# A decoder layer with an expert ring on one Trainium2 core: a constants tensor narrowed by 96 columns, and the working memory moved to a start at a multiple of 512 bytes

## The chip, the cores and the metric

The kernel runs on one core of a Trainium2 chip. The metric is the device time of one execution in microseconds. Three executions of the kernel before took 1125.96 us as the median, 1125.75 us the shortest and 1127.47 us the longest.

## The reference

The reference is one layer of a hybrid decoder for 256 tokens of width 1024, in float32. Three branches are computed from one projection of the normalised input (a sparse attention of 8 heads with an indexer that picks 64 keys per query, an RWKV-7 time mixing of 8 heads, and a cross-attention into 256 memory tokens), merged by sigmoid gates and added to the input. Then comes the part in which the kernel spends more than half of its time, a feed-forward layer of 16384 single-neuron experts. For each token and each of 8 heads it picks 16 experts, 128 per token:

```python
def peer_ffn(xn, w_q, key1, key2, u, v):
    q = (xn @ w_q).reshape(B, S, PEER_HEADS, 2, PEER_QDIM // 2)
    s1 = jnp.einsum('bshd,kd->bshk', q[..., 0, :], key1)     # 128 keys
    s2 = jnp.einsum('bshd,kd->bshk', q[..., 1, :], key2)
    v1, i1 = lax.top_k(s1, 16); v2, i2 = lax.top_k(s2, 16)
    cand = v1[..., :, None] + v2[..., None, :]
    sc, ci = lax.top_k(cand.reshape(..., 256), 16)
    expert = e1 * PEER_KEYS + e2                             # from i1, i2 at ci
    gate = jax.nn.softmax(sc, axis=-1)
    ue, ve = u[expert], v[expert]                            # rows of 1024
    hid = jax.nn.gelu(jnp.einsum('td,ted->te', xn, ue))
    return jnp.einsum('te,ted->td', gate * hid, ve)
```

## The kernel before, in words

The program has two stages. In the first, TensorE works through the projections: 51 weight blocks of 1 MB each, loaded by SyncE into a ring of three buffers (`wring`) and a few spare places, and between them the small matmuls of the three branches, in an order written out by hand (`SCHEDULE`). The blocks are used by `channels` (L610), `tokens` (L623) and `up` (L959); all are matmuls of 128x128 weights with 256 columns.

In the second stage (heads 0 to 7 of the experts, for two tiles of 128 tokens) the unit of work is one gather. GpSimd issues an indirect DMA (L1835) that fetches for each of the 128 tokens one row of the table `experts`, in which `u` and `v` of an expert stand side by side: 2048 floats, 8192 bytes, into that token's partition of one of 8 slots. There are 16 experts x 8 heads x 2 tiles = 256 such gathers. When one has landed, VectorE makes the dot product of the `u` half with the token (L1769, in place), ScalarE the gelu (L1265), the product with the gate (L1269) and a diagonal matrix of the weights (L1272), and TensorE multiplies that with the `v` half and sums in PSUM (L991). Then the slot is free (`group_free`) and GpSimd issues the next gather into it. Between the dots VectorE chooses the experts of the next head.

No pool hands out the memory. Each tensor is allocated once, one behind the other in every partition, in the order of the code: `const`, `vec`, `trig`, `lora`, `glora`, `rows`, `small`, `ones`, `pos_i`, `pool_mem`. Each start is rounded up to a multiple of 32 bytes, and `const` starts at byte 16512. The last one, `pool_mem` (47872 columns of float32), holds everything else: the function `part(at, ...)` cuts tiles from it by hand, with `K1 = 256` columns as the unit, so that the weight buffers, the slots of the ring of rows (`slot`) and the output buffer (`o_sb`) all begin at a multiple of 1024 bytes from its start:

```python
RING0 = Q0 + 16 * K1
slot = [part(RING0 + BLOCK * i, BLOCK) for i in range(SLOTS)]
```

`const` holds the constant matrices side by side; `CONST[name]` is the pair of first column and width by which `c(name)` finds them. Two of them, `pick_pairs` and `pick_ones`, serve the sums of squares (`square_sums`, L642 to L645). Each is 224 columns wide, with the values in columns 96 to 127 and zeros left and right, and the four matmuls of a sum read windows of 128 columns that start at 96, 64, 32 and 0. `small` holds single columns, of which the first 144 are used.

Of the kernel before, what the change touches and what calls it, by code (L numbers as in the profile page):

```python
# [13 lines left out]
P = 128  # L14
# [53 lines left out]

CONST = {}
_c = 0  # L70
for _name, _n in [("ident", 128), ("headsel", 2), ("pick_pairs", 224), ("pick_ones", 224), ("rot", 128), ("causal", 128),
                  ("gram_mask", 4 * CHUNK), ("level", CHUNK * LEVELS), ("iota", 16), ("inv_freq", 1), ("two_idents", CHUNK), ("to_heads", W)]:
    CONST[_name] = (_c, _n)
    _c += _n
CONST_COLS = _c


VEC = {}
# [8 lines left out]
def constants():  # L87

    p = np.arange(P)
    out = {}  # L90
    out["ident"] = np.eye(P)
    out["pick_pairs"] = np.zeros((P, 224))
    out["pick_pairs"][:, 96:128] = p[:, None] // HD == np.arange(32)[None, :] // 16
    out["pick_ones"] = np.zeros((P, 224))
    out["pick_ones"][:, 96:128] = 1.0
    out["to_heads"] = p[:, None] == 16 * (np.arange(W)[None, :] // HD)
    out["two_idents"] = np.concatenate([np.eye(64), np.eye(64)])
    rot = np.zeros((P, P))
    for base in (0, HD):
        for i in range(8):  # L100
            rot[base + 8 + i, base + i] = -1.0
            rot[base + i, base + 8 + i] = 1.0
    out["rot"] = rot
    out["causal"] = np.where(p[None, :] <= p[:, None], 0.0, OFF)
    s, t = p[:, None] % CHUNK, np.arange(CHUNK)[None, :]
    strict, incl = s < t, s <= t
    out["gram_mask"] = np.concatenate([strict, incl, strict, incl], axis=1)
    out["level"] = np.concatenate(
        [(s // (2 << l) == t // (2 << l)) & ((t >> l) % 2 == 1) & ((s >> l) % 2 == 0) for l in range(LEVELS)], axis=1)
    out["headsel"] = (p[:, None] // HD == np.arange(2)[None, :])  # L110
    out["iota"] = np.tile(np.arange(16), (P, 1))
    inv = (np.float32(1.0) / (np.float32(500000.0) ** (np.arange(0, 16, 2, dtype=np.float32) / np.float32(16))))
    col = np.zeros(P)
    for q in range(P):
        if q % HD < 16:
            col[q] = inv[(q % HD) % 8]
    out["inv_freq"] = col[:, None]
    return np.ascontiguousarray(np.concatenate([out[n] for n in CONST], axis=1).astype(np.float32))
# [87 lines left out]
def build(nc, t_in, out):  # L206
    ctx = ExitStack()
    with ctx:
        def sb(name, shape, dt=F32):
            return ctx.enter_context(nc.sbuf_tensor(name, shape, dt))  # L210
# [4 lines left out]

        const = sb("const", [P, CONST_COLS])
        vec = sb("vec", [P, VEC_COLS])
# [1 line left out]
        lora = sb("lora", [P, W])  # L219
        glora = sb("glora", [P, W])  # L220
        rows = sb("rows", [P, 2 * W])
        small = sb("small", [P, 160])
        ones = sb("ones", [P, P])
        pos_i = sb("pos_i", [P, S], I32)
        pool_mem = sb("pool_mem", [P, POOL_COLS])
# [146 lines left out]
        def c(name):  # L372
            a, n = CONST[name]
            return const[:, a:a + n]
# [5 lines left out]
        ident = c("ident")  # L380
# [1510 lines left out]
```

## Time and profile before

| | |
|---|---|
| median of 3 runs | 1125.96 us |
| the profiled execution | 1125.06 us |
| its span, first to last instruction | 1123.2 us |
| TensorE (PE) busy | 879.6 us, 78% |
| VectorE (DVE) busy | 649.7 us, 58% |
| ScalarE (ACT) busy | 392.9 us, 35% |
| GpSimd (POOL) busy | 324.7 us, 29% |
| DMA | 329.78 MB, mean 294 GB/s |
| queue of the gathers (q0) | 36864 packets, 268.45 MB, 57.7% of 16 engines |
| mean granted TensorE clock | 0.848 |

The table is of the profiled execution except for its first line. Shares of the span are averages over two stages that have different limits, so they don't tell what bounds the kernel; the windows below do. A queue's share is the time that its packets took on the 16 DMA engines, as a part of 16 times the span or window. A packet here is one row, or the write of a semaphore at a transfer's end. Neighbouring packets overlap a little, and a share can pass 100%. Windows are in us from the start of the span.

### The profile page before, as it was taken

The page shows a single profiled execution, that of the slowest core. Times are in us where ns is not written, and L with a number is a line of the kernel's source. Part 1 is how long each engine was busy: PE and PEld are TensorE (multiplying, and loading weights), DVE is VectorE, ACT ScalarE, POOL GpSimd, SP SyncE. Part 2 cuts the span into 40 slices and gives each one's busy share as a digit, 9 for nine tenths or more (in the row PEclk, how much of TensorE's full clock was granted, in tenths as well). Part 3 has the DMA queues.
Part 4 walks back from the last instruction along what each step waited for, and adds up shares of the span by engine and source line. Part 5 has one row for each costly group of instructions (what it writes and reads, how often), then busy time and mean ns, then how long its engine had stood idle before and what let it go on. Part 6 is the DMA issues. An engine that isn't in the chain of part 4 may idle for free.

```text
span 1123.2 us, 16457 instructions
## 1 busy us (share of the span) xinstructions
PE 879.6 (78%) x5738; PEld 518.5 (46%) x5738; DVE 649.7 (58%) x1544; ACT 392.9 (35%) x1094; POOL 324.7 (29%) x294
## 2 busy tenths in 40 slices
PE   9999999999999989988856566565565667656655
PEld 8888888878888878855411111111111111111111
DVE  3442541296453241666577668668757766766874
ACT  2024133315321101244454344344434434434443
POOL 0000000020011000225444545454544454445441
PEclk9999999999999999999985866777667566667677
DMA  8343423322222254789999999999999999999997
GB/s 321 135 150 113 146 79 113 113 76 76 76 76 78 76 211 148 298 332 404 421 420 422 420 422 422 421 422 421 421 421 422 421 422 422 422 422 421 422 422 290
DMA packets 46579, 329.78 MB, mean 294 GB/s; under 512 B 5312, under 2 KB 5568, under 8 KB 6848
## 3 DMA queue, kind: packets, MB, share of 16 engines
q0 software_dynamic: 36864, 268.45, 57.7%
q1 hardware_dynamic: 9104, 58.91, 14.5%
q10 hardware_dynamic: 560, 1.70, 0.4%
q8 instruction: 36, 0.59, 0.2%
q14 instruction: 15, 0.12, 0.0%
HBM read 328.00 MB, written 1.05 MB: 293 GB/s over the span
## 4 chain that ended last, share of the span: by engine, by line
PE 48%; DMA 27%; DVE 11%; ACT 7%; issue 6%; POOL 1%; POOLq 0%; DVEq 0%; ACTq 0%
DMA pool_mem<-in_experts,pool_mem 27%; PE psum_proj L610 20%; PE psum_job L991 8%; PE psum_proj L623 5%; DVE pool_mem L1769 4%; PE psum_proj L959 3%; PE psum_job L839 3%; ACT L1265 1%; DVE pool_mem L1710 1%; ACT L1253 1%; POOL pool_mem L1835 1%; ACT pool_mem L1272 1%; ACT pool_mem L1269 1%; DVE pool_mem L1707 1%; PE psum_proj L1014 1%
## 5 line engine op out<-in xcount | busy, mean ns | idle before, releaser
L991 PE MATMUL psum_job<-pool_mem 64*64 64x512 f32 x2048 | 378.2, 849 | 222.6 <-ACT pool_mem L1272 222.4
L1835 POOL DMA_INDIRECT pool_mem<-in_experts,pool_mem x256 | 302.5, 1182 | 444.3 <-PE psum_job L991 286.0
L1769 DVE CUSTOM_DVE_ANT_0 pool_mem<-pool_mem 128x1024 f32<-128x1024 f32 x256 | 310.5, 1225 | 188.0 <-DMA pool_mem<-in_experts,pool_mem 186.8
L991 PEld LDWEIGHTS psum_job<-pool_mem 64*64 64x64 f32 x2048 | 86.4, 172 | 510.3 <-issue 509.9
L610 PE MATMUL psum_proj<-pool_mem 128*128 128x256 f32 x1120 | 247.9, 380 | 0.7 <-ACT pool_mem L1085 0.7
L610 PEld LDWEIGHTS psum_proj<-pool_mem 128*128 128x128 f32 x1120 | 211.1, 190 | 33.8 <-issue 5.9
L1265 ACT ACTIVATE pool_mem<-pool_mem 128x1 f32<-128x1 f32 x256 | 51.6, 202 | 291.3 <-DVE pool_mem L1769 290.7
L1818 POOL TENSOR_TENSOR pool_mem<-pool_mem,const 128x256 f32<-128x256 f32 x24 | 16.7, 716 | 332.9 <-DVE pool_mem L1573 273.1
L1272 ACT ACTIVATE pool_mem<-const,pool_mem 128x64 f32<-128x64 f32 x256 | 89.1, 348 | 26.5 <-PE psum_job L991 0.6
L1269 ACT ACTIVATE pool_mem<-pool_mem 128x1 f32<-128x1 f32 x256 | 75.4, 294 | 9.3
L623 PE MATMUL psum_proj<-pool_mem 128*128 128x256 f32 x256 | 56.3, 380 | 1.6 <-DVE pool_mem L1653 1.6
L623 PEld LDWEIGHTS psum_proj<-pool_mem 128*128 128x128 f32 x256 | 48.4, 190 | 8.3 <-DVE pool_mem L1653 2.0
L959 PE MATMUL psum_proj<-pool_mem 128*128 128x256 f32 x192 | 43.5, 383 | 0.7 <-ACT pool_mem L1203 0.7
L959 PEld LDWEIGHTS psum_proj<-pool_mem 128*128 128x128 f32 x192 | 35.8, 190 | 6.1 <-ACT pool_mem L1203 0.9
L1117 ACT ACTIVATE pool_mem<-psum_proj,vec 128x256 f32<-128x256 f32 x24 | 10.1, 470 | 75.5 <-PE psum_proj L610 75.5
L1328 DVE RECIPROCAL pool_mem<-pool_mem 128x256 f32<-128x256 f32 x5 | 8.6, 1739 | 47.8 <-ACT pool_mem L1058 45.8
L839 PE MATMUL psum_job<-pool_mem 64*64 64x64 f32 x896 | 30.0, 220 | 1.4 <-issue 0.6
L839 PEld LDWEIGHTS psum_job<-pool_mem 64*64 64x64 f32 x896 | 27.8, 135 | 4.6 <-issue 4.3
L1253 ACT ACT_TABLE_LOAD x17 | 21.8, 1283 | 2.0 <-DVE pool_mem L1733 1.7
L1265 ACT ACT_TABLE_LOAD x17 | 21.8, 1283 | 0.3
L1585 DVE TENSOR_TENSOR pool_mem<-pool_mem,psum_job 128x256 f32<-128x256 f32 x36 | 13.9, 419 | 12.5 <-PE psum_job L839 11.5
L1769 DVE DVE_READ_ACCUMULATOR2_ANT pool_mem<- 128x1 f32 x256 | 21.0, 82 | 0.0
(250 smaller groups left out, 731.5 us busy)
## 6 DMA issues: line engine op xcount, KB each, us to landing
pool_mem<-in_weights SPq DMA_DIRECT2D x51, 1024.0 KB, 4.8
pool_mem<-in_experts,pool_mem POOLq DMA_INDIRECT x256, 14.0
const<-in_const SPq DMA_DIRECT2D x1, 1033.5 KB, 15.0
pool_mem<-in_xT SPq DMA_DIRECT2D x1, 1024.0 KB, 4.9
pool_mem<-in_memT SPq DMA_DIRECT2D x1, 1024.0 KB, 11.2
pool_mem<-in_x ACTq DMA_DIRECT2D x1, 1024.0 KB, 7.6
rows<-in_rows SPq DMA_DIRECT2D x1, 512.0 KB, 16.6
pool_mem<-in_ffn_gain ACTq DMA_DIRECT2D x1, 512.0 KB, 8.3
```

The source lines that it names most:

```text
L610: ins = mm(o[:, m, :], lhsT=w[:, k, m * P:(m + 1) * P], rhs=src[:, k, :], start=(k == 0), stop=(k == KT - 1))
L623: ins = mm(o[:, t, :], lhsT=src[:, k, t * P:(t + 1) * P], rhs=w[:, k, :], start=(k == 0), stop=(k == KT - 1))
L839: ins = mm(o[b, CHUNK * i:CHUNK * i + CHUNK], lhsT=left[b, 4 * g + i, :], rhs=c("two_idents")[b] if right is None else right[b, 4 * g + i, ...
L959: ins = mm(o[:, m, :], lhsT=w[:, 4 * (u % 2) + k, m * P:(m + 1) * P], rhs=ys[u // 4][:, k, :], start=(k == 0), stop=(k == 3))
L991: ins = mm(sum_bank(t, d)[sum_strip(i, d), :], lhsT=diag[rows_, g % DIAGS, :], rhs=slot[g % SLOTS][rows_, D + 512 * d:D + 512 * d + 512], ...
L1253: A(gate_e[:, par, :], top[:, par, :], ACT.Exp, bias=gstat[:, par, 0:1], accum_out=gstat[:, par, 1:2]).then_inc(sg["gsum"], 1)
L1265: A(act_h[:, par, col], hid[:, par, col], ACT.Gelu).then_inc(sg["gelu_ok"], 1)
L1269: A(weight[:, par, col], act_h[:, par, col], ACT.Copy, scale=gate_e[:, par, col]).then_inc(sg["weighed"], 1)
L1272: A(diag[:, g % DIAGS, :], c("two_idents"), ACT.Copy, scale=weight[:, par, col]).then_inc(sg["diag_ok"], 1)
L1769: ins = V.tensor_tensor_reduce(u, u, xn_tok[:, t, :], 1.0, 0.0, ALU.mult, ALU.add, hid[:, par, s_:s_ + 1])
L1818: G_.tensor_tensor(LmT[:, gs, :], gram[:, gs, 0, :], level.unsqueeze(1).to_broadcast([P, 4, CHUNK]), ALU.mult).then_inc(sg["lm_ok"], 1)
L1835: G_.indirect_dma_start(slot[s_ % SLOTS], None, t_in["experts"], bass.IndirectOffsetOnAxis(ap=expert_i[:, par, s_:s_ + 1], axis=0)).then_i ...
```

## The change

The matrix `pick_pairs` takes up 128 columns of `const` in place of 224. Its zeros on the right are no longer stored: `pick_ones` stands right behind it and begins with 96 zero columns, and the entry of `CONST` is widened to 224 again after the columns have been counted. `const` shrinks from 2067 to 1971 columns. `small` grows from 160 to 208 columns, and the added ones aren't used. No instruction is added, removed or moved. The starts of the tensors in each partition, in bytes, by the widths and the rounding to 32:

| | before | after |
|---|---|---|
| `const` | 16512 | 16512 |
| `vec` | 24800 | 24416 |
| `trig` | 25152 | 24768 |
| `lora` | 27200 | 26816 |
| `glora` | 29248 | 28864 |
| `rows` | 31296 | 30912 |
| `small` | 35392 | 35008 |
| `ones` | 36032 | 35840 |
| `pos_i` | 36544 | 36352 |
| `pool_mem` | 37568 = 73 x 512 + 192 | 37376 = 73 x 512 |

```diff
--- before.py
+++ after.py
@@ -68,11 +68,12 @@
 
 CONST = {}
 _c = 0
-for _name, _n in [("ident", 128), ("headsel", 2), ("pick_pairs", 224), ("pick_ones", 224), ("rot", 128), ("causal", 128),
+for _name, _n in [("ident", 128), ("headsel", 2), ("pick_pairs", 128), ("pick_ones", 224), ("rot", 128), ("causal", 128),
                   ("gram_mask", 4 * CHUNK), ("level", CHUNK * LEVELS), ("iota", 16), ("inv_freq", 1), ("two_idents", CHUNK), ("to_heads", W)]:
     CONST[_name] = (_c, _n)
     _c += _n
 CONST_COLS = _c
+CONST["pick_pairs"] = (CONST["pick_pairs"][0], 224)
 
 
 VEC = {}
@@ -89,7 +90,7 @@
     p = np.arange(P)
     out = {}
     out["ident"] = np.eye(P)
-    out["pick_pairs"] = np.zeros((P, 224))
+    out["pick_pairs"] = np.zeros((P, 128))
     out["pick_pairs"][:, 96:128] = p[:, None] // HD == np.arange(32)[None, :] // 16
     out["pick_ones"] = np.zeros((P, 224))
     out["pick_ones"][:, 96:128] = 1.0
@@ -219,7 +220,7 @@
         lora = sb("lora", [P, W])
         glora = sb("glora", [P, W])
         rows = sb("rows", [P, 2 * W])
-        small = sb("small", [P, 160])
+        small = sb("small", [P, 208])
         ones = sb("ones", [P, P])
         pos_i = sb("pos_i", [P, S], I32)
         pool_mem = sb("pool_mem", [P, POOL_COLS])
```

## Rows read from the trace of the kernel before

**Rows 1.** Windows by stage; columns are named in the first line.

```profile
core 0: us, PE busy (x) PEld busy (x) DVE busy (x) ACT busy (x) POOL busy (x), PEclk, DMA share, GB/s
0.00:466.00 466.00, 450.80 (x3435) 390.08 (x3436) 197.26 (x407) 115.00 (x221) 23.30 (x40) 1.00 0.36 129
466.00:1115.00 649.00, 426.02 (x2288) 127.84 (x2288) 450.52 (x1134) 276.35 (x869) 301.41 (x255) 0.74 1.00 415
1115.00:1123.20 8.20, 2.77 (x16) 0.57 (x16) 1.93 (x3) 1.51 (x5) 0.00 (x0) 0.71 0.23 65
```

**Rows 2.** Page, part 2, DMA in 40 slices of the span.

```profile
DMA  8343423322222254789999999999999999999997
GB/s 321 135 150 113 146 79 113 113 76 76 76 76 78 76 211 148 298 332 404 421 420 422 420 422 422 421 422 421 421 421 422 421 422 422 422 422 421 422 422 290
```

**Rows 3.** DMA queues and issues, 600 to 1100 us.

```profile
q0 software_dynamic: 28870, 210.23, 101.0%
...
issues: line engine op xcount, KB each, median us to landing
pool_mem<-in_experts,pool_mem POOLq DMA_INDIRECT x200, 14.6
```

**Rows 4.** Waits, 600 to 1100 us.

```profile
engine line waited for: us in total, times, longest us
...
ACT pool_mem L1265 <- DVE pool_mem L1769: 256.3, 174, 3.9
POOL pool_mem L1835 <- PE psum_job L991: 221.5, 119, 4.6
...
DVE pool_mem L1769 <- DMA pool_mem<-in_experts,pool_mem: 134.3, 111, 1.3
```

**Rows 5.** DMA issues of the whole span: KB each, median us to landing.

```profile
pool_mem<-in_weights SPq DMA_DIRECT2D x51, 1024.0 KB, 4.8
...
const<-in_const SPq DMA_DIRECT2D x1, 1033.5 KB, 15.0
...
pool_mem<-in_x ACTq DMA_DIRECT2D x1, 1024.0 KB, 7.6
...
pool_mem<-in_ffn_gain ACTq DMA_DIRECT2D x1, 512.0 KB, 8.3
...
pool_mem<-in_keysT ACTq DMA_DIRECT2D x1, 128.0 KB, 8.2
```

**Rows 6.** Windows, steady part of the second stage.

```profile
600.00:1100.00 500.00, 311.86 (x1608) 69.15 (x1600) 357.42 (x909) 211.89 (x670) 239.20 (x200) 0.69 1.01 422
```

**Rows 7.** Tile const, 0 to 120 us: duration ns min/median/max, first and last start.

```profile
L645 PE MATMUL psum_job<-pool_mem,const x24: 379/379/454, 90.7 to 115.2; 128*128 128x256 f32 x24
...
L532 SPq DMA_DIRECT2D const<-in_const x1: 443/443/443, 3.9 to 3.9; - x1
L1368 DVE TENSOR_SCALAR trig<-trig,const x1: 353/353/353, 69.3 to 69.3; 128x256 f32<-128x256 f32 x1
```

**Rows 8.** Waits of PE, 0 to 476 us, the longest two.

```profile
PE psum_job L819 <- DVE pool_mem L1553: 2.2, 2, 1.1
PE psum_proj L623 <- DVE pool_mem L1653: 1.6, 1, 1.6
```

**Rows 9.** DMA queues, 403.5 to 409.2 us.

```profile
q10 hardware_dynamic: 560, 1.70, 74.4%
```

**Rows 10.** DMA queues, 803.5 to 811.5 us.

```profile
q1 hardware_dynamic: 303, 0.52, 17.2%
```

**Rows 11.** DMA queues, 15.7 to 17 us.

```profile
DMA packets 71, 0.56 MB, mean 432 GB/s; under 512 B 3, under 2 KB 3, under 8 KB 3
...
q1 hardware_dynamic: 71, 0.56, 102.5%
```

**Rows 12.** Page, part 5, the matmuls of 128x256 on pool_mem.

```profile
L610 PE MATMUL psum_proj<-pool_mem 128*128 128x256 f32 x1120 | 247.9, 380 | 0.7 <-ACT pool_mem L1085 0.7
...
L623 PE MATMUL psum_proj<-pool_mem 128*128 128x256 f32 x256 | 56.3, 380 | 1.6 <-DVE pool_mem L1653 1.6
...
L959 PE MATMUL psum_proj<-pool_mem 128*128 128x256 f32 x192 | 43.5, 383 | 0.7 <-ACT pool_mem L1203 0.7
```

## The prediction

> **What bounds the kernel now.** I read the windows by stage first, then the slices of the page, the DMA queues of a steady window, the waits of the same window, and last the rows of single transfers.
>
> The windows by stage [rows 1] show two programs one behind the other. Up to 466 us TensorE is busy 450.80 of 466 us at a granted clock of 1.00, and DMA is busy a third of the time: this stage is bound by TensorE. From 466 to 1115 us the share of the DMA engines is 1.00 and TensorE is busy 426 of 649 us. In the slices [rows 2] the GB/s stand at 420 to 424 from slice 18 on, with no dip: a resource at its cap. The last 8.2 us, from the last landing to the end, are dots, a matmul, a copy and a store.
>
> The second stage is the 256 gathers of expert rows (L1835). Each writes 128 rows of 8192 bytes, 1.0486 MB, into one of 8 slots of the ring. At 422 GB/s [rows 3] that is 2.485 us, and 256 x 2.485 = 636 us, all but 13 us of the stage. The waits [rows 4] agree: the dots on VectorE wait 134.3 us for the gathers' data, ScalarE waits for the dots, and GpSimd for a slot to come free. Such a loop of waits could also be a latency loop. What excludes it is the time from issue to landing: 14.6 us for a gather in the steady window [rows 3], against 4.8 us for a weight load of the same 1 MB alone in the queue [rows 5]. So a gather stands about 10 us in the queue behind others, and the engines could be slower by that much per slot before the DMA engines ran dry. By throughput VectorE has 357.42 of 500 us used and TensorE 311.86 [rows 6].
>
> So in the first stage a change counts if TensorE's matmuls change, and in the second only if the time of a DMA row changes.
>
> **The change part by part.** No engine gets another instruction, another order or another wait. What changes are the start addresses and the width of one load.
>
> 1. Addresses. The program's tensors stand one behind the other in each partition, each start rounded up to 32 bytes; `const` begins at byte 16512. By the widths of the code, `pool_mem` begins before at 37568 = 73 x 512 + 192, afterwards at 37376 = 73 x 512. All that is cut from it as a whole tile lies at a multiple of 1024 bytes from that start, so before the change each row of the ring, and of each weight block, begins 192 bytes past a multiple of 512 (and of 256); afterwards each begins at a multiple of 512. Every other tensor moves by 384 or 192 bytes, both multiples of 64, so nothing changes for what an engine sees within 64 bytes.
>
> 2. The load of `const` is 96 columns narrower: 128 x 384 bytes = 49 KB less of 1033.5 KB. At 422 GB/s that is 0.12 us less in front of the lora weights, the rows and the fourth weight block. `const` lands 15.0 us after its issue at 3.9 us and is first read at 69.3 us [rows 5, 7]; the longest total wait of TensorE up to 476 us is 2.2 us, for VectorE and not for a load [rows 8]. The cover is some 50 us deep: cost and gain 0. If that cover were gone, 0.12 us.
>
> 3. The shared zero columns. The four matmuls of each sum of squares read the same 128-column weights from `const`, with the same values (the last 96 columns of the `pick_pairs` window are now the first of `pick_ones`, zeros). L645 keeps its count and its 379 ns [rows 7]: 0.
>
> 4. What the 192 bytes cost a DMA row. This is the only term that can matter: 256 gathers x 128 rows / 16 engines = 2048 rows on each engine one behind the other, so 1 ns of a row is 2.05 us of the kernel. The trace has only the old place of `pool_mem`, so I ask how much of a packet's time isn't the bytes. In the steady window q0 has 28870 packets and 210.23 MB in 101.0% of 16 x 500 us = 8080 us. For the three late loads that ScalarE issues (q10, rows of 4096 and 1024 bytes: 560 packets, 1664 KB = 1.704 MB by their issues) it is 74.4% of 16 x 5.7 us = 67.9 us [rows 3, 5, 9]. Time = packets x f + bytes / r for both gives f = 7 ns and r = 26.7 bytes per ns. So a row of 8192 bytes is 307 ns of bytes and 7 ns that don't depend on size. Both groups go to `pool_mem`, so a price per 256 or 512 bytes crossed could still sit in r; a price per row sits in f.
>
> Is f, or a part of r, the price of the 192 bytes? Two rows say no. Stores of the first half of the output (q1 in 803.5 to 811.5 us, rows of 2048 bytes read from `pool_mem`): 17.2% of 128 us = 22.0 us for 303 packets and 0.52 MB [rows 10]; bytes at 26.7 take 19.6 us, which leaves 8 ns a packet, and 47 of the 303 are semaphore packets with 4 bytes, which cross no boundary. And the load of `const` itself, whose rows go to a start 128 bytes past a multiple of 256 and come from rows of 8268 bytes that begin anywhere in HBM: 71 packets, 0.56 MB in 102.5% of 16 x 1.3 us = 21.3 us [rows 11], 38.1 us per MB against 38.4 in the ring, equal within the rounding of 0.56. Three offsets (192 written, 192 read, 128 written from scattered starts), one price.
>
> The bounds of term 4: the nearest gain is all of f on the rows, 7 ns x 2048 = 14.3 us. The far one is the highest rate in any short window, 432 GB/s in that of `const`: 256 x 1.0486 MB at 432 in place of 422 is 621 for 636 us, 15 us, the same size. A loss is bounded by the same distance the other way, since nothing here shows a row dearer than those of the ring: 15 us at most, with nothing that speaks for it. I take 0, to which the rows on stores and on `const` are nearest.
>
> The Trainium skill speaks against my choice here ("DMA: Bandwidth & Descriptors", How a descriptor splits into AXI transactions): a descriptor that doesn't start at a multiple of 256 bytes first fetches the bytes from the boundary below, which cost beats. It says so of reads; the experts' rows are 8192 bytes wide and so begin aligned in HBM, and the stores, where SBUF is the side read, show no such extra. Carried over to writes it would be the rival A below. The same page (Where 436 GB/s comes from) puts the ceiling of the ports at 435.2 GB/s; if alignment alone led there from 422, the 636 us would shrink by 19 us, and the time be 1106.
>
> 5. What the addresses cost the engines. Matmuls 128x256 f32 take 380 ns with both operands in `pool_mem` (L610, L623) and 383 ns at L959 [rows 12]; with the weights in `const`, which begins at another offset, the median is 379 [rows 7]. So the place of an operand is worth -1 to +3 ns. I take 0. In the second stage engine times hide under the transfers (10 us, above).
>
> The sum: 0 + 0 + 0 + 0 + 0. The profiled execution took 1125.06 us (span 1123.2 and 1.9 around it), 0.9 under the median of the runs, 1125.96. So the profile of after should read 1123 and the median 1125.9.
>
> **The rivals.**
>
> A. A row that begins 192 bytes off carries those bytes, or one more transaction, and loses them now. 192 bytes at 26.7 bytes per ns are 7.2 ns, all of f: 2048 x 7.2 = 14.7 us, 1111 us. With one part-filled transaction more, say 2 to 3 ns, 4 to 6 us: 1121. For it: the second stage is bound by nothing else for 636 us, a gain would pass through (VectorE would go from 71% to 73% busy), and f in fact equals 192 bytes. Against it: the semaphore packets, the stores and the const rows.
>
> B. The row does get cheaper at the SBUF end, and something else sets its pace. The slots don't: 0.06 us less per gather against the 10 us that a gather spends in the queue. It would have to be the reading end, the memory with the experts: then a row stays at 310 ns, 1125.9. It differs from the forecast in cause and not in time.
>
> C. Slower: TensorE's operand reads get worse at the new starts. Place: the first stage, where TensorE is 97% busy and each ns is paid in full. Price: the 3 ns between L610 and L959 on 1120 + 256 + 192 matmuls of that shape, 4.7 us: 1130.7 us. It decides from 1.5 ns a matmul on (2.3 us). For it only that such a spread exists; against it the 379 ns with weights from `const`.
>
> D. The change does not do what it says, and `pool_mem` isn't at a multiple of 512 afterwards. By the sums of the widths it is. No time of its own: 1125.9.
>
> **How the numbers follow.** Forecast, with B and D, 0.69: 1125.9, own range 1124.2 to 1127.8 (the three runs before span 1125.75 to 1127.47). A in full 0.07 (1111), A in part 0.13 (1117 to 1123). C 0.11 (up to 1130.7). A measurement of this kernel can tell about 0.2%, 2.3 us. Faster by more than that: 0.07 + 0.13 = 0.20. Slower: C, 0.11. Within: 0.69. The range reaches down into the partial A, to 1119, and up into C, to 1128.5; it leaves out A in full, the lower end of A in part and the upper half of C, just under 0.2.
>
> **What would show it.** Right: q0 in 600 to 1100 us again near 28870 packets, 422 GB/s and 101% share; 14.6 us to landing; L610 at 380 ns; the stages cut at 466 and 1115 us. Rival A: more packets in the same window (a gather is 2485 - 8 x 7 = 2429 ns, so 28870 x 2485/2429 = 29540 for the whole of f), 432 GB/s, and the last landing ahead of 1115. C: the first gather later than 466 us, with L610 above 381 ns. Wrong altogether would be a q0 rate that moves by over 0.5% either way, for I take the place of the rows to be worth nothing.

## The result: 8 us less, and the profile after

The kernel after takes 1118.50 us (median of 4 runs, 1117.58 to 1119.20), the kernel before 1126.51 us (4 runs, 1125.75 to 1127.47). The ratio is 0.9928, with a 95% interval from 0.9911 to 0.9945: 0.7% faster. The forecast range ended at 1119.0, half a microsecond above. The profiled execution took 1118.73 us, its span is 1116.9 us.

The slices of the page of after, to be read against [rows 2]: the steady level of the DMA engines has gone from 420 to 422 up to 425 to 428 GB/s, and up to 466 us the mean is 129 GB/s in both. The slices there differ in detail, since they are a little narrower after and a load can fall on the other side of a cut.

```profile
DMA  8343323322211253789999999999999999999997
GB/s 324 133 151 113 137 90 113 114 71 82 77 63 67 100 188 136 275 346 396 427 426 427 428 428 427 427 428 427 425 428 426 426 428 427 427 427 427 427 427 290
```

The DMA queues and issues of after in 600 to 1100 us (packets, MB, share of 16 engines) answer to [rows 3]:

```profile
DMA packets 29557, 213.58 MB, mean 427 GB/s; under 512 B 3299, under 2 KB 3299, under 8 KB 3555
...
q0 software_dynamic: 29246, 212.96, 100.8%
...
pool_mem<-in_experts,pool_mem POOLq DMA_INDIRECT x201, 13.6
```

29246 packets passed where 28870 did, in a share that is 0.2 points smaller, and a gather lands after 13.6 us and not 14.6. That is a cheaper row and not a fuller queue: 500 us / 213.58 MB x 1.0486 MB (the bytes of a gather) is 2455 ns. The same window of before moved 210.84 MB in all (the stores included), so 2487 ns. The difference is 32 ns over 8 rows of an engine, 4.0 ns a row, and 4.0 x 2048 = 8.2 us, the measured gain.

The windows by stage of after, cut where its last gather landed, answer to [rows 1]:

```profile
core 0: us, PE busy (x) PEld busy (x) DVE busy (x) ACT busy (x) POOL busy (x), PEclk, DMA share, GB/s
0.00:466.00 466.00, 450.82 (x3432) 389.80 (x3433) 197.19 (x407) 114.52 (x220) 22.12 (x38) 1.00 0.36 129
466.00:1109.00 643.00, 428.85 (x2295) 128.42 (x2297) 449.69 (x1135) 276.82 (x870) 311.10 (x256) 0.73 1.00 419
1109.00:1116.90 7.90, 2.10 (x16) 0.37 (x16) 1.88 (x3) 1.43 (x4) 0.00 (x0) 0.84 0.23 67
```

The second stage takes 643 us by these cuts in place of 649. From the issue of its first gather to the landing of the last it is 642.9 us (466.0 to 1108.9) where it was 650.7 (464.6 to 1115.3): 7.8 us less. The span fell by only 6.3 in this pair of profiles because the first stage ended 1.4 us later. The `up` matmuls, 383 ns in [rows 12], ran 394 ns there:

```profile
L611 PE MATMUL psum_proj<-pool_mem 128*128 128x256 f32 x1120 | 247.9, 380 | 0.7 <-ACT pool_mem L1086 0.7
...
L624 PE MATMUL psum_proj<-pool_mem 128*128 128x256 f32 x256 | 56.3, 380 | 1.6 <-DVE pool_mem L1654 1.6
...
L960 PE MATMUL psum_proj<-pool_mem 128*128 128x256 f32 x192 | 45.2, 394 | 0.7 <-ACT pool_mem L1204 0.7
```

It isn't the addresses. The longest of the 192 took 631 ns against 483 before, at the same median of 379, and the granted clock in 402 to 405 us was 0.61, so for part of these 3 us it was at the lower level, 1.2 GHz in place of 2.4. In before it was 1.00 there, although TensorE was busy 3.7 of the 6 us ahead of it in both. Of the runs below, e1, f2, f3 and f6 show the same 394 ns. The others show 383, and among them is g3, whose tensors stand where those of after do.

### The profile page after: what moved, and what is told of

It reads as the page before. It is cut to its first block, busy times and chain, and to the rows that moved or that the text cites. A ratio compares the mean times of both kernels' runs of the same rounds, so it can differ in the third digit from the quotient of the medians.

```text
span 1116.9 us, 16457 instructions
## 1 busy us (share of the span) xinstructions
PE 881.8 (79%) x5738; PEld 518.6 (46%) x5738; DVE 648.8 (58%) x1544; ACT 392.8 (35%) x1094; POOL 333.2 (30%) x294
## 4 chain that ended last, share of the span: by engine, by line
PE 46%; DMA 35%; DVE 7%; issue 5%; ACT 5%; POOL 0%; POOLq 0%; ACTq 0%; DVEq 0%
DMA pool_mem<-in_experts,pool_mem 35%; PE psum_proj L611 20%; PE psum_job L992 5%; PE psum_proj L624 5%; PE psum_proj L960 3%; DVE pool_mem L1770 3%; PE psum_job L840 3%; ACT pool_mem L1273 1%; DVE pool_mem L1711 1%; ACT pool_mem L1270 1%; PE psum_proj L1015 1%; PE psum_job L631 1%; DVE pool_mem L1708 1%; PE psum_job L640 1%; PE psum_job L660 1%
## 5 line engine op out<-in xcount | busy, mean ns | idle before, releaser
L1836 POOL DMA_INDIRECT pool_mem<-in_experts,pool_mem x256 | 311.1, 1215 | 431.0 <-PE psum_job L992 269.5
```

Of the source, the lines that this page charges most:

```text
L1836: G_.indirect_dma_start(slot[s_ % SLOTS], None, t_in["experts"], bass.IndirectOffsetOnAxis(ap=expert_i[:, par, s_:s_ + 1], axis=0)).then_i ...
```

## The experiments

The diffs below are against the kernel after and show the lines that matter; `...` marks lines that are left out. The ratios and intervals are those on record and can differ by 0.1% from the quotient of the medians that stand beside them. The theory after the comparison was W: in a long stream of rows, one that doesn't begin at a boundary in the partition costs the writing side a fixed amount more. The rivals were: the cost grows with the bytes below the boundary (P), the other tiles' places (E) or the narrower constants (C) brought the gain, only GpSimd's queue pays (Q), and only a meeting with the engines' accesses costs (E2).

### e1_zeros_only: the shared zeros without the boundary

```diff
-        small = sb("small", [P, 208])
+        small = sb("small", [P, 160])
```

> The shared zero columns alone: small stays at 160 columns, so pool_mem begins at 37184 = 72 x 512 + 320, 64 bytes past a multiple of 256. Theory W (a ring row that doesn't begin at a boundary costs the write side a fixed amount more once the queues have been full for some 10 us): the narrower constants do nothing, and since the rows still begin off the boundary the time is that of before, 1126.5, with q0 at 422 GB/s in 600 to 1100 us and 14.6 us to landing. Theory P (the extra cost grows with the bytes below the boundary, here 64 in place of 192): a third of the cost stays, 8.0 / 3 = 2.7 us, so about 1121.2 and 425 to 426 GB/s. Theory C (the narrower const or any moved address is what helped): 1118.5.

Measured: 1127.34 us (10 runs) against 1126.97 (19 runs) of before, ratio 0.9998 (0.9985 to 1.0012). The narrower constants are worth nothing: C falls. The steady window shows the level of before, although the rows now stand 64 bytes past a multiple of 256 and not 192, so P falls as it was put, with a boundary of 256 or 512:

```profile
DMA packets 29177, 210.83 MB, mean 422 GB/s; under 512 B 3254, under 2 KB 3254, under 8 KB 3510
...
q0 software_dynamic: 28866, 210.22, 101.0%
```

### e2_base_256: a multiple of 256 that is none of 512

```diff
-        small = sb("small", [P, 208])
+        small = sb("small", [P, 144])
```

> As after, but small has 144 columns: pool_mem begins at 37120 = 72 x 512 + 256. If the boundary that counts is 256 bytes, the time is that of after, 1118.5 us at 427 GB/s. If it is 512 bytes, theory W gives 1126.5 at 422 GB/s, and a cost by the bytes below the 512 boundary would give more than before (256 against 192), about 1129.

Measured: 1118.77 us (4 runs), ratio to before 0.9928 (0.9901 to 0.9954), the time of after. A multiple of 256 suffices. Whether a multiple of 128 would do was not tried, since every ring off the boundary in these runs begins 64 or 80 bytes past one:

```profile
DMA packets 29558, 213.61 MB, mean 427 GB/s; under 512 B 3296, under 2 KB 3296, under 8 KB 3552
...
q0 software_dynamic: 29247, 213.00, 100.8%
```

### e3_ring_alone_on and e4_ring_alone_off: which tiles count

e3 has `small` of 160 columns, with `pool_mem` at 72 x 512 + 320. e4 has `small` of 208, with `pool_mem` at 73 x 512. Both have:

```diff
-POOL_COLS = 187 * 256
+POOL_COLS = 187 * 256 + 48
...
-        RING0 = Q0 + 16 * K1
+        RING0 = Q0 + 16 * K1 + 48
```

> pool_mem begins at 37184 (320 past a multiple of 512), but the 8 slots of the ring are moved by 48 columns = 192 bytes, so that they alone begin at a multiple of 512. Theory W: only the ring's rows count, 1118.5 us and 427 GB/s. Theory E (tiles that the engines read and write beside the transfers, such as xn_tok, diag or the choice's tiles, must stand well): the time of e1, near 1126.

> The reverse: pool_mem begins at a multiple of 512 as in after, the ring's slots alone stand 192 bytes past one. Theory W: the whole gain is gone, 1126.5 us and 422 GB/s. Theory E: 1118.5.

Measured: e3 1118.28 us (4 runs), ratio 0.9913 (0.9892 to 0.9934). e4 1126.64 us (10 runs), ratio 0.9999 (0.9987 to 1.0011). The slots of e3 stand at the bytes of those of after, those of e4 at the bytes of those of before, while the rest of `pool_mem` is off the boundary in e3 and on it in e4. So the 8 slots alone carry the whole effect in both directions: E falls. The steady windows of e3 and, behind it, of e4:

```profile
DMA packets 29553, 213.59 MB, mean 427 GB/s; under 512 B 3293, under 2 KB 3293, under 8 KB 3549
...
q0 software_dynamic: 29242, 212.98, 100.8%
```

```profile
DMA packets 29182, 210.87 MB, mean 422 GB/s; under 512 B 3255, under 2 KB 3255, under 8 KB 3511
...
q0 software_dynamic: 28871, 210.25, 101.0%
```

### f1_sp_off and f2_sp_on: plain loads from SyncE

```diff
...
-                        G_.indirect_dma_start(slot[s_ % SLOTS], None, t_in["experts"],
-                                              bass.IndirectOffsetOnAxis(ap=expert_i[:, par, s_:s_ + 1], axis=0)
-                                              ).then_inc(slot_in[s_ % SLOTS], 16)
...
+            for n in range(PEER_HEADS * TILES):
+                sp.wait_ge(sg["experts_ok"], n + 1)
+                for s_ in range(TOPK):
+                    sp.wait_ge(sg["group_free"], n * HEAD_GROUPS + s_ + 1)
+                    sp.dma_start(slot[s_ % SLOTS], t_in["experts"][P * s_:P * s_ + P, :]).then_inc(slot_in[s_ % SLOTS], 16)
```

The loops and the wait around GpSimd's call go with it. f1 has the ring moved by 48 columns as in e4, f2 has it as in after.

> The ring's slots 192 bytes past a multiple of 512 (as in e4), and the 256 gathers replaced by plain loads that SyncE issues, each of the same 128 consecutive rows of the table for a place in the ring; the rows fetched are not the chosen ones, and both stores wait to the end. It asks whether the cost belongs to GpSimd's indirect DMAs or to any queue that is kept full. Theory W (any long stream of rows off the boundary pays, short bursts don't because the write side can fall some 100 ns behind first): the steady rate is 422 GB/s, rows of 312 to 319 ns. Theory Q (only the software queue pays): 427 GB/s and 309 ns as in every weight load of before.

> f1 with the ring at a multiple of 512. Both theories: 427 GB/s and rows of 309 ns; what counts is the difference to f1: W 1.2% in the steady rate, Q none.

Measured, one run each, so that the level of the steady window decides and not the time: f1 1122.80 us, f2 1116.00 us. The steady windows, f1 and then f2:

```profile
DMA packets 28942, 210.83 MB, mean 422 GB/s; under 512 B 3212, under 2 KB 3212, under 8 KB 3212
...
q1 hardware_dynamic: 28934, 210.73, 101.3%
```

```profile
DMA packets 29328, 213.63 MB, mean 427 GB/s; under 512 B 3256, under 2 KB 3256, under 8 KB 3256
...
q1 hardware_dynamic: 29320, 213.53, 101.1%
```

422 against 427 GB/s in a hardware queue whose source rows lie one behind the other: Q falls. Neither the software queue nor the scattered rows are needed for the cost.

### f3_lean_off: engines that hardly touch the ring

```diff
-                    u = slot[s_ % SLOTS][:, 0:D]
+                    u = slot[s_ % SLOTS][:, 0:64]
...
-                                 rhs=slot[g % SLOTS][rows_, D + 512 * d:D + 512 * d + 512],
+                                 rhs=slot[g % SLOTS][rows_, D + 512 * d:D + 512 * d + 64],
...
```

The token's side of the dot and the sum in PSUM are narrowed in the same way, and the ring stands as in e4.

> e4 (ring off the boundary) with engines that hardly touch the ring: the dots run over 64 of 1024 columns and the matmuls over 64 of 512, so most of each expert is left out of the sum. Theory W: q0 stays at 422 GB/s, the time at 1126 or little under it (the shorter tail, 2 us). Theory E2 (a row off the boundary is only dearer where it meets reads and writes of the engines): q0 goes up to 427 GB/s, the time to 1118 or below.

Measured, one run: 1125.32 us. The windows of f3 in 600 to 1100 us show TensorE's busy time at 99 of 500 us where it was 312 [rows 6], VectorE's at 163 where it was 357, and the GB/s in the last column the same:

```profile
600.00:1100.00 500.00, 99.17 (x1600) 67.41 (x1600) 162.96 (x909) 211.13 (x667) 187.32 (x200) 0.50 1.01 422
```

E2 falls: the cost is whole, 422 GB/s, with most of the engines' work on the ring gone. The time is 1.3 us under the median of e4 and inside e4's ten runs (1124.77 to 1129.11), with two thirds of TensorE's work gone; that says again what bounds the stage.

### f6_ring_208: a start inside 32 bytes

```diff
-        RING0 = Q0 + 16 * K1
+        RING0 = Q0 + 16 * K1 + 52
```

(and `POOL_COLS` 52 larger; the rest as after)

> After with the ring's slots alone 208 bytes past a multiple of 512, which is 16 bytes past a multiple of 32. Theory W in its simplest form (one more transaction per row, whatever the offset) gives 1126.5 us and 422 GB/s. If a start inside 32 bytes costs one beat more in each row, one beat of 32 bytes at 26.7 bytes per ns is 1.2 ns, 2.5 us: 1129. If every transaction of 256 bytes is hit, 32 x 1.2 ns a row, 38 ns: 1126 + 79 = 1205.

Measured: 1128.16 us (10 runs), ratio 1.0014 (1.0005 to 1.0024) to before.

```profile
DMA packets 29080, 210.11 MB, mean 420 GB/s; under 512 B 3245, under 2 KB 3245, under 8 KB 3501
...
q0 software_dynamic: 28769, 209.50, 101.0%
```

210.11 MB are 2495 ns a gather, 9 ns more than e4's 2486: 1.1 ns a row, 2.3 us. That agrees in size with one beat more per row (1.2 ns), and a price on every transaction (38 ns a row) is excluded.

Another reading fits as well and was not tested. The rows of before, e1 and e4 begin 64 bytes past a multiple of 128 and those of f6 80 bytes past one. A price in proportion to these bytes would be 4.0 x 80 / 64 = 5.0 ns a row in f6, and it measures 4.0 + 1.1 = 5.1. Rings that begin 32, 128 and 224 bytes past a multiple of 256 would tell a fixed price per row from one by such bytes.

### g1_sp_half_off and g2_sp_half_on: per row or per byte

Against f1 and f2:

```diff
-                    sp.dma_start(slot[s_ % SLOTS], t_in["experts"][P * s_:P * s_ + P, :]).then_inc(slot_in[s_ % SLOTS], 16)
+                    for d in range(2):
+                        sp.dma_start(slot[s_ % SLOTS][:, D * d:D * d + D],
+                                     t_in["experts"][P * s_:P * s_ + P, D * d:D * d + D]).then_inc(slot_in[s_ % SLOTS], 16)
```

VectorE waits for twice the count of a slot's semaphore, 32 in place of 16.

> As f1 (plain loads from SyncE in place of the gathers, ring 192 bytes off, the rows not the chosen ones), but each load is cut in two of 128 rows x 4096 bytes. From f1 and f2: a row of 8192 takes 309.6 ns off and 305.7 ns on the boundary; less 301 ns for the bytes, by the packets of both sizes, that is 4.5 ns a packet and 4 ns for the offset. Theory W (per row): 16 rows of 150.5 + 4.5 + 4 = 159 ns and 2 semaphore packets of 9 ns, 2562 ns for 1.0486 MB, 409 GB/s. If the 4 ns belong to the bytes or to each boundary passed (32 per row of 8192, 16 per row of 4096): 157 ns, 2530 ns, 414 GB/s.

> g1 with the ring at a multiple of 512: 16 x 155 + 18 = 2498 ns, 420 GB/s by both. The distance to g1 tells: 2.6% if the cost is per row, 1.3% if it is per byte or boundary.

Measured, one run each: g1 1142.45 us, g2 1127.81 us. The steady windows, g1 and then g2:

```profile
DMA packets 56202, 204.73 MB, mean 409 GB/s; under 512 B 6244, under 2 KB 6244, under 8 KB 56192
...
q1 hardware_dynamic: 56192, 204.61, 102.6%
```

```profile
DMA packets 57622, 209.90 MB, mean 420 GB/s; under 512 B 6400, under 2 KB 6400, under 8 KB 57612
...
q1 hardware_dynamic: 57612, 209.79, 102.6%
```

409 and 420 GB/s, as W gave them: 2561 less 2498 ns over 16 rows is 3.9 ns a row of 4096 bytes, as much as for one of 8192. The price is per row and doesn't grow with its length. The halved rows themselves cost 2455 to 2498 ns, 1.7%.

### g3_source_off: the start in HBM

```diff
-        "experts": np.concatenate([a["peer_u"][0], a["peer_v"][0]], axis=1),
+        "experts": np.concatenate([a["peer_u"][0], a["peer_v"][0], np.zeros((128 * 128, 16), np.float32)], axis=1),
```

> After (ring on the boundary), with the table of experts padded to 2064 columns, of which 2048 are fetched: its rows then begin 0, 64, 128 or 192 bytes past a multiple of 256 in HBM, a quarter each. Theory W (the write side is what sets the pace, and only its start counts): 427 GB/s, 1118.5 us. If the reading side pays for the bytes below the boundary, as a page's rule has it, the mean of 96 bytes at 26.7 bytes per ns is 3.6 ns a row, 7.4 us: 422 to 423 GB/s and 1125.9 us. If any start off the boundary costs the reading side the same 4 ns, three rows in four pay: 3 ns, 6.1 us, 1124.6.

Measured: 1119.19 us (4 runs), ratio to before 0.9934 (0.9913 to 0.9956): the time of after.

```profile
DMA packets 29555, 213.60 MB, mean 427 GB/s; under 512 B 3295, under 2 KB 3295, under 8 KB 3551
...
q0 software_dynamic: 29244, 212.98, 100.8%
```

Where a row starts in HBM costs nothing here, with the ring at a multiple of 512. That the writing side hides a price of the reading side is theory W's reading; no run shows which side sets the pace once the ring stands well. The rule of the Trainium skill ("DMA: Bandwidth & Descriptors", How a descriptor splits into AXI transactions), by which a read pays for the bytes below the boundary, doesn't show: its 3.6 ns a row would have been 422 to 423 GB/s. Carried over to the written side, with its boundary of 256, it doesn't fit as an amount by bytes either: e1 (64 bytes off) and e4 (192) both have 422. One transaction more for a row that crosses, its table's count for such a start, would fit e1 and e4; that is an inference, since no view shows transactions.

## Why the prediction was wrong, point by point

**What bounds the kernel** was right. Terms 2, 3 and 5 were right too: the zeros and the narrower load are worth 0 (e1), the matmuls kept 380 ns, and the second stage followed the row in full. One reading of [rows 2] was off without effect: the slice of 404 GB/s is ahead of the steady level, which is 420 to 422 and begins with the next one.

**Term 4 failed**, the price of the 192 bytes on a DMA row, at "I take 0": it is 4.0 ns a row, and 2048 rows make 8.2 us of it. A fixed price per row of about this size stood among the rivals as A in part, "one part-filled transaction more, say 2 to 3 ns"; it got 0.13. Its size of 4.0 ns put the time below the range too. The argument for 0 ("three offsets, one price") rested on rows that couldn't show the price. The stores [rows 10] read from `pool_mem` and so never write to the place in question. They, the `const` load [rows 11] and the late loads [rows 9] are short trains of rows, and in a short train the record of a packet is the same on and off the boundary. Here is the hardware queue around one weight load of 1 MB (297.6 to 301.6 us), in the kernel before, in after, in e1 (off the boundary) and in e2 (on it):

```profile
q1 hardware_dynamic: 144, 1.05, 73.4%
```

```profile
q1 hardware_dynamic: 144, 1.05, 73.4%
```

```profile
q1 hardware_dynamic: 144, 1.05, 75.1%
```

```profile
q1 hardware_dynamic: 144, 1.05, 74.5%
```

That before and after have the same 73.4% is chance. It is 366 ns a row in the mean, because some of the first rows after the issue have records of up to 1.1 us, and 4 ns a row would be 0.8 points, less than the spread of these four. The trace's single records settle it: the median row of this load is 309 ns in before and in after. In the steady window 8% of the rows of before have a record of 310 ns or less, and over 99% of those of after. Off the boundary the price comes into the record only when the stream has run full for a while. In before, q0 in 478 to 488 us and in 560 to 570 us:

```profile
q0 software_dynamic: 552, 3.99, 95.0%
```

```profile
q0 software_dynamic: 577, 4.20, 101.0%
```

95.0% of 160 us over 552 packets, 65 of them semaphores of 9 ns, is 311 ns a row; 101.0% over 577 with 64 is 314 ns. In after the same windows (586 packets in 101.2%, 583 in 100.7%) give 309 and 309 to 310. Why short trains don't show it is not settled: that the writing side lags behind its own records until something is full is my reading, and no run tested it.

The second error was the fit of f and r. It took one group from the full stream and one from short loads, and put the extra of the full stream into the wrong terms. What f caught is there on the boundary too: the median records of after are 9 ns for a semaphore and 84, 159 and 309 ns for rows of 2048, 4096 and 8192 bytes, which is 9 ns and 75 ns per 2048 bytes. That f came out at 192 bytes' worth was chance, since 64 bytes cost the same. The trace of before did have the difference, 314 ns for a row of the ring against 309 for one of a weight load. It would have led to A. The one other cause at hand was the kind of queue, and f1 shows that the kind is none.

**The rivals.** A in full (1111) is excluded by 4.0 ns for 7.2. B, a cheaper row with the pace set elsewhere, is excluded too, for the pace followed the row. C had nothing in it: e2, e3 and e4 kept 383 ns at three starts. D was no case. The signs named ahead of the run were right: more packets in the same window and an earlier last landing were to mean A, and they came.

## What to carry to other kernels

In a stage that DMA bounds with row after row into SBUF, put the start of the destination in each partition at a multiple of 256 bytes: 48 columns of offset were worth 4.0 ns a row, 1.3% of rows of 8192 bytes and 2.5% of rows of 4096, the first in either kind of queue, and the source's start was worth nothing. The price is per row, so its share grows as rows get shorter. And don't take a steady price from short transfers: compare rates of the long stream, or run the one with the start moved.

## What the runs showed that I had not expected

- A multiple of 256 bytes suffices, not only the 512 that the change aims at (e2, 1118.77 us), and it is needed for the ring alone (e3, 1118.28 us). A start 128 bytes past such a multiple is untested. Widening `small` isn't needed: with 144 columns, fewer than before, the place is as good.
- The price is the same 4.0 ns at 64 and at 192 bytes past a multiple of 256, and 1.1 ns more at 208 (f6). Whether the further 1.1 ns come from a start inside 32 bytes or from 80 bytes past a multiple of 128 in place of 64 is open.
- The records of short trains hide it: the rows of a weight load are 309 ns in the median on and off the boundary, while those of the ring are 309 ns on it and 314 off it.
